# One 512-column product over w hi and w lo in the v units of a float32r decoder layer

## The chip, the cores and the metric

One core of a Trainium2 chip runs the whole kernel. The metric is device time in microseconds (us), the median of several executions of the same program; lower is better.

## What is computed

The reference is one pre-norm decoder layer on 256 tokens of width 1024, in float32 (depth is 1, so only mixer A runs; with 256 tokens there is one block, and its attention is plain causal attention with a T5 relative-position bias):

```
y = rmsnorm(h, norm_mix)
q, k, v = split(y @ w_in, 3)              # [256, 1024] @ [1024, 3072], 16 heads of 64
s = q k^T / 8 + bias(distance), causal
h = h + softmax(s) v @ w_out              # [256, 1024] @ [1024, 1024]
y = rmsnorm(h, norm_mlp)
h = h + square(relu(y @ mlp_up)) @ mlp_down   # 4096 hidden
out = rmsnorm(h, final_norm)
```

## The kernel before, in words

TensorE multiplies in float32r, a shortened float32. To keep float32 accuracy every operand of a large product is split into a high part (the value rounded to float32r) and a low part (the rest), and three products are summed: hi by hi, hi by lo, lo by hi. For the weights, 1 MB tiles are loaded into `raw` (4 slots), ScalarE copies each half of a tile to `w_hi` (`hi_tile`, line 494), and VectorE subtracts to give `w_lo` (`lo_tile`, line 672). Loads into a slot are issued by SyncE once the `lo` of the slot's previous tile is done.

The work is written out by hand, one instruction stream for each engine, tied together by semaphores. The in-projection is cut into 4 chunks of 4 heads (256 columns of each of q, k and v), numbered c = 0 to 3. Chunk 0 runs v, q, k; the others run q, k, v, with the attention of chunk c - 1 between them (scores, softmax, transposes, values). Each part of a chunk is one weight tile and two "units". The q and k units (`feature_unit`, lines 297 and 298) hold a block of weights still and stream the transposed activations `yT`, whose hi and lo halves lie side by side: for each of the 8 blocks k of 128 rows, one matmul of 512 columns (w hi against y hi and y lo) and one of 256 (w lo against y hi). The bank then holds two halves; ScalarE copies the second half to `part` (`qk_part`, line 532) and VectorE adds it to the first (`qk_sum`, line 733).

The v units (`v_unit`, lines 280 to 282) are the other way round: a block of `yT` is held still and the weights stream, 256 columns each time, so they take three matmuls for each k, all into the first 256 columns of the bank. ScalarE alone empties that bank:

```
nc.scalar.copy(v_sb[:, tb, :], bank[UNIT[tb]][:, 0:CW]).then_inc(v_ready, 1)   # v_copy, line 527
```

Both kinds of unit alternate between bank 0 and bank 1 (`UNIT`). Before a unit writes its bank, `unit_free` waits until the unit that used the bank last has been read: `v_ready` after a v unit, `qk_ready` after a q or k unit. So the first q unit of chunk 0 waits for `v_ready` to be 1, and the second for 2. The attention's `values` and the out-projection wait for `v_ready` too.

In chunk 0 TensorE runs, after the first norm: `transposes(0, 0)` (line 250), the v unit of token block 0 with `transposes(0, 1)` inside it, the v unit of token block 1, the small product of the bias table (line 423, 384 columns on 32 rows), and then four q and k units. VectorE runs there, in this order: `lo_tile(1, 0)`, `lo_tile(1, 1)`, `lo_tile(2, 0)`, the bias vector `bv_sb` (line 831, which waits for the product of line 423), `lo_tile(2, 1)`, `lo_tile(3, 0)`, `qk_sum(0, "q", 0)`, and so on. ScalarE runs `hi_tile(1, 0)`, `hi_tile(1, 1)`, `hi_tile(2, 0)`, `v_copy(0, 0)`, `hi_tile(2, 1)`, `v_copy(0, 1)`. In chunks 1 to 3 the v units come last and `scores(c)` right behind them; VectorE's next work is `add_bias` (line 742) of these scores, the start of the softmax. After chunk 3 comes the out-projection (`mix`), then the MLP, both with 512-column products at line 342 and units as above.

Of the kernel before, what the change touches and what calls it, by code (L numbers as in the profile page):

```python
# [27 lines left out]
F32R = mybir.dt.float32r  # L28
ALU = mybir.AluOpType
ACT = mybir.ActivationFunctionType  # L30

P = 128
D = 1024
T = 256
TB = T // P
KB = D // P
# [4 lines left out]
CW = 256  # L41
# [3 lines left out]
CE = D * CW // P  # L45
HALF = CE // 2
SLOTS = 4
# [10 lines left out]
HI, LO = 0, 1  # L58
# [18 lines left out]
def build(nc, x, rel_bias, norm_mix, norm_mlp, mlp_up, mlp_down, w_in, w_out, final_norm,  # L77
# [9 lines left out]
    with ExitStack() as ctx:  # L87
        def sb(name, shape, dt=F32):
            return ctx.enter_context(nc.sbuf_tensor(name, shape, dt))

        def sem(name):
            return ctx.enter_context(nc.semaphore(name))
# [3 lines left out]
        y_sb = sb("y_sb", [P, TB, D])  # L96
        yT = sb("yT", [P, KB, 2, T], F32R)
        raw = sb("raw", [P, SLOTS, CE])
        w_hi = sb("w_hi", [P, SLOTS, CE], F32R)
        w_lo = sb("w_lo", [P, SLOTS, CE], F32R)  # L100


        qT = sb("qT", [P, 2, T])
# [1 line left out]
        v_sb = sb("v_sb", [P, TB, CW])  # L105
# [4 lines left out]
        part = sb("part", [P, 2, T])  # L110
# [19 lines left out]
        bank = [ctx.enter_context(nc.psum_tensor(f"bank{i}", [P, 512], F32)) for i in range(8)]  # L130
        UNIT = [0, 1]
# [20 lines left out]
        unit_done, v_ready, part_done, qk_ready = sem("unit_done"), sem("v_ready"), sem("part_done"), sem("qk_ready")  # L152
        scores_done, biased, exp_done = sem("scores_done"), sem("biased"), sem("exp_done")
        rinv_done, normed = sem("rinv_done"), sem("normed")
        pt_done, pt_ready = sem("pt_done"), sem("pt_ready")
        pv_done, othi_done, ot_ready = sem("pv_done"), sem("othi_done"), sem("ot_ready")
        mix_done, wout_used, h_done = sem("mix_done"), sem("wout_used"), sem("h_done")
# [7 lines left out]
        def cols(slot_tensor, slot):  # L165
            return slot_tensor[:, slot, :].rearrange("p (k n) -> p k n", k=KB)

        def rows(slot_tensor, slot):
            return slot_tensor[:, slot, :].rearrange("p (k n) -> p k n", k=2)


        def unit_of(c, part):
            return 2 * IN_PARTS.index((c, part))
# [66 lines left out]
        def _(pe):  # L240
            mm = nc.tensor.matmul

            def transposes(norm, tb):

                if norm == 0 and tb == 0:
                    pe.wait_ge(ident_loaded, 16)
                for b in range(2):
                    pe.wait_ge(y_done, 2 * (norm * TB + tb) + b + 1)
                    for k in range(4):
                        last = nc.tensor.transpose(bank[NORM[tb][b]][:, k * P:(k + 1) * P],  # L250
                                                   y_sb[:, tb, (4 * b + k) * P:(4 * b + k + 1) * P], ident[:])
                    last.then_inc(yt_done, 1)

            def unit_free(n):

                if n < 2:
                    return
                c, part = IN_PARTS[n // 2 - 1]
                if part == "v":
                    pe.wait_ge(v_ready, 2 * c + n % 2 + 1)  # L260
                else:
                    pe.wait_ge(qk_ready, 4 * c + 2 * (part == "k") + n % 2 + 1)

            def v_unit(c, tb, first=False):

                n = unit_of(c, "v")
                slot = n // 2 % SLOTS
                if not first:
                    pe.wait_ge(lo_done, n + 2)
                    unit_free(n + tb)  # L270
                wh, wl = cols(w_hi, slot), cols(w_lo, slot)
                acc = bank[UNIT[tb]][:, 0:CW]
                tok = slice(tb * P, (tb + 1) * P)
                for k in range(KB):
                    if first and k % 4 == 0:
                        pe.wait_ge(ylo_done, 2 * tb + k // 4 + 1)
                        if k and tb == 0:
                            transposes(0, 1)
                        pe.wait_ge(lo_done, k // 4 + 1)
                    mm(acc, yT[:, k, HI, tok], wh[:, k, :], start=(k == 0), stop=False)  # L280
                    mm(acc, yT[:, k, HI, tok], wl[:, k, :], start=False, stop=False)  # L281
                    last = mm(acc, yT[:, k, LO, tok], wh[:, k, :], start=False, stop=(k == KB - 1))  # L282
                last.then_inc(unit_done, 1)

            def qk_unit(c, part, i):
# [129 lines left out]
            for b in range(2):  # L415
                last = mm(bank[GAIN[b]][:], ones[:], gain[0:1, b * 512:(b + 1) * 512], start=True, stop=True)
# [69 lines left out]
        def _(act):  # L486
# [9 lines left out]
            def hi_tile(t, half):  # L496

                hi(t % SLOTS, half, 16 * (t // SLOTS + 1), (unit_done, 2 * (t - SLOTS) + 2) if t >= SLOTS else None)
# [23 lines left out]
                    nc.scalar.copy(yT[:, 4 * b:4 * b + 4, HI, tb * P:(tb + 1) * P],  # L522
                                   bank[NORM[tb][b]][:].rearrange("p (k n) -> p k n", k=4)).then_inc(yhi_done, 1)

            def v_copy(c, tb):
                act.wait_ge(unit_done, unit_of(c, "v") + tb + 1)
                nc.scalar.copy(v_sb[:, tb, :], bank[UNIT[tb]][:, 0:CW]).then_inc(v_ready, 1)

            def qk_part(c, part_, i):

# [51 lines left out]
            for half in range(2):  # L582
                hi_tile(1, half)
            hi_tile(2, 0)
            v_copy(0, 0)
            hi_tile(2, 1)
            v_copy(0, 1)
            hi_tile(3, 0)
            qk_part(0, "q", 0)
            hi_tile(3, 1)  # L590
# [7 lines left out]
            for c in range(1, CHUNKS_IN):  # L598
                a, t = c - 1, 3 * c + 3
                if c == 1:  # L600
                    hi_tile(t, 0)
                    qk_part(c, "q", 0)
                softmax_exp(a, 0)
                softmax_exp(a, 1)
                softmax_exp(a, 2)
                if c > 1:
                    qk_part(c, "q", 0)
                softmax_exp(a, 3)
                if c > 1:
                    hi_tile(t, 0)  # L610
                qk_part(c, "q", 1)
                hi_tile(t, 1)
                hi_tile(t + 1, 0)
                qk_part(c, "k", 0)
                hi_tile(t + 1, 1)
                qk_part(c, "k", 1)
                out_hi(a, 0)
                out_hi(a, 1)
                hi_tile(t + 2, 0)
                hi_tile(t + 2, 1)  # L620
                v_copy(c, 0)
                v_copy(c, 1)

            a = CHUNKS_IN - 1
            for head in range(4):
# [36 lines left out]
        def _(dve):  # L662
            v = nc.vector
# [11 lines left out]
            def lo_tile(t, half):  # L675
                lo(t % SLOTS, half, 2 * t + half)
# [52 lines left out]
            def qk_sum(c, part_, i):  # L729
# [3 lines left out]
                v.scalar_tensor_tensor(dst, bank[UNIT[i]][:, 0:T], -SCALE if part_ == "q" else 1.0, part[:, i, :],  # L733
                                       ALU.mult, ALU.add).then_inc(qk_ready, 1)

            def add_bias(a, s):

                if s == 0:
                    dve.wait_ge(bias_loaded, a * 16 + 16)
                dve.wait_ge(scores_done, 4 * a + s + 1)  # L740
                for tb, own, bias in ((0, slice(0, P), slice(P, T)), (1, slice(P, 3 * P), slice(0, T))):
                    last = v.tensor_tensor_reduce(probs[:, s, own], bank[SCORE[s]][:, own], bias_sb[:, s, bias],  # L742
                                                  1.0, MASKED, ALU.add, ALU.min,
                                                  negmax[:, s, tb:tb + 1])
                last.then_inc(biased, 1)
# [80 lines left out]
            for half in range(2):  # L826
# [3 lines left out]
            dve.wait_ge(bias_summed, 1)  # L830
            v.scalar_tensor_tensor(bv_sb[:], bank[BIAS][0:HEADS, 0:BV], -1.0, fill_sb[:], ALU.mult, ALU.add
                                   ).then_inc(bias_vec, 1)
            lo_tile(2, 1)
            lo_tile(3, 0)
            qk_sum(0, "q", 0)
            lo_tile(3, 1)
# [7 lines left out]
            for c in range(1, CHUNKS_IN):  # L844
                a, t = c - 1, 3 * c + 3
                if c == 1:
                    lo_tile(t, 0)
                    softmax(a, c)
                else:
                    softmax(a)  # L850
                    qk_sum(c, "q", 0)
                softmax_rest(a)
                if c > 1:
                    lo_tile(t, 0)
                qk_sum(c, "q", 1)
                if c == 1:
                    lo_tile(t, 1)
                    qk_sum(c, "k", 0)
                    pT_copy(a, 0)
                    pT_copy(a, 1)  # L860
                    lo_tile(t + 1, 0)
                    qk_sum(c, "k", 1)
                    pT_copy(a, 2)
                    pT_copy(a, 3)
                else:
                    pT_copy(a, 0)
                    pT_copy(a, 1)
                    lo_tile(t, 1)
                    qk_sum(c, "k", 0)
                    pT_copy(a, 2)  # L870
                    pT_copy(a, 3)
                    lo_tile(t + 1, 0)
                    qk_sum(c, "k", 1)
                lo_tile(t + 1, 1)
                out_lo(a, 0)
                out_lo(a, 1)
                lo_tile(t + 2, 0)
                lo_tile(t + 2, 1)
            a = CHUNKS_IN - 1
            softmax(a)  # L880
            softmax_rest(a)
# [63 lines left out]
```

## Time and profile before

| | |
|---|---|
| median of 3 runs | 316.43 us (315.7 to 316.58) |
| span of the profiled execution, first to last instruction | 314.9 us |
| own time of the profiled execution | not given apart from its span |
| TensorE matmuls | busy 301.6 us (96% of the span), 1686 instructions |
| VectorE | busy 208.9 us (66%), 398 instructions |
| ScalarE | busy 160.7 us (51%), 293 instructions |
| DMA | 55.94 MB, mean 178 GB/s |

The span is shorter than the time by what lies around the first and the last instruction, about 1.5 us against the median. A busy time is the sum of an engine's instructions without overlaps; which of them set the end is told by the chain of waits, not by the share.

### The profile page before, as it was taken

To read this page: it belongs to the slowest core of one execution; us is meant where nothing else is said; L and a number is where in the kernel's file an instruction comes from. 1 tells how busy PE (TensorE), PEld (TensorE's weight loads), DVE (VectorE), ACT (ScalarE), POOL (GpSimd) and SP (SyncE) were. 2 spreads that over 40 slices of the span, in tenths; PEclk is the share of its full clock that TensorE was granted. 3 is DMA by queue.
4 is the path that set the end of the run, shared out by engine and by line. 5 is a ranking of instruction groups with operands and counts; after the bars stand their busy time and mean duration, and the time that the engine had idled before them with its cause. 6 is when DMAs were issued, how large, how long until landed. Compare 5 with 4: busy or idle time off the path is not lost.

```text
span 314.9 us, 4661 instructions
## 1 busy us (share of the span) xinstructions
PE 301.6 (96%) x1686; PEld 255.2 (81%) x1686; DVE 208.9 (66%) x398; ACT 160.7 (51%) x293; POOL 6.5 (2%) x14
## 2 busy tenths in 40 slices
PE   5699999999999999899999999999999999999992
PEld 2688888889889878898888888888888888888881
DVE  3677797675875849866855675585476558547554
ACT  2494584644744736454554464354446436444422
POOL 2002000000000000000000000000000000000000
PEclk9999999999999999999999999999999999999997
DMA  6989957455348034645656465645745556530003
GB/s 204 359 266 354 319 197 258 153 178 204 138 133 256 13 133 136 200 135 186 213 169 233 159 216 158 213 187 146 252 148 206 180 191 208 137 129 0 2 1 133
DMA packets 36592, 55.94 MB, mean 178 GB/s; under 512 B 1073, under 2 KB 29905, under 8 KB 36578
## 3 DMA queue, kind: packets, MB, share of 16 engines
q1 hardware_dynamic: 35586, 52.50, 50.9%
q0 software_dynamic: 992, 3.25, 3.2%
q8 instruction: 9, 0.15, 0.2%
q14 instruction: 5, 0.04, 0.0%
HBM read 54.67 MB, written 1.07 MB: 177 GB/s over the span
## 4 chain that ended last, share of the span: by engine, by line
PE 90%; DVE 4%; DMA 2%; ACT 2%; issue 1%; SPq 0%; DVEq 0%; ACTq 0%
PE bank L342 35%; PE bank L297 26%; PE bank L298 13%; PE bank L280 3%; PE bank L281 3%; PE bank L282 3%; DMA raw<-in_a_w_in_dram 2%; PE bank L380 1%; PE bank L318 1%; PE bank L381 1%; PE bank L332 1%; DVE w_lo L672 1%; PE bank L250 1%; PE bank L310 1%; PE bank L308 1%
## 5 line engine op out<-in xcount | busy, mean ns | idle before, releaser
L672 DVE TENSOR_TENSOR w_lo<-raw,w_hi 128x1024 fp32r<-128x1024 f32 x96 | 115.1, 1220 | 60.4 <-ACT w_hi L494 57.6
L297 PE MATMUL bank<-yT,w_hi 128*128 128x512 f32 x368 | 131.6, 400 | 0.1
L494 ACT CAST w_hi<-raw 128x1024 fp32r<-128x1024 f32 x95 | 96.8, 1048 | 53.1 <-PE bank L342 53.1
L298 PE MATMUL bank<-yT,w_lo 128*128 128x256 f32 x368 | 103.2, 280 | 0.0
L297 PEld LDWEIGHTS bank<-yT,w_hi 128*128 128x128 f32 x368 | 69.1, 188 | 18.4 <-issue 1.3
L342 PE MATMUL bank<-w_hi,hT 128*128 128x512 f32 x256 | 71.8, 390 | 0.0
L298 PEld LDWEIGHTS bank<-yT,w_lo 128*128 128x128 f32 x368 | 69.5, 189 | 0.5
L342 PEld LDWEIGHTS bank<-w_hi,hT 128*128 128x128 f32 x256 | 47.0, 188 | 9.7
L342 PE MATMUL bank<-w_lo,hT 128*128 128x512 f32 x128 | 40.2, 390 | 0.0
L342 PEld LDWEIGHTS bank<-w_lo,hT 128*128 128x128 f32 x128 | 24.0, 188 | 5.2
L553 ACT COPY part<-bank 128x256 f32<-128x256 f32 x30 | 11.2, 373 | 23.3 <-PE bank L298 23.3
L280 PE MATMUL bank<-w_hi,yT 128*128 128x256 f32 x64 | 19.5, 305 | 2.4 <-DVE yT L724 2.4
L342 PE MATMUL bank<-w_hi,oT 128*128 128x512 f32 x64 | 19.2, 398 | 0.0
L281 PE MATMUL bank<-w_lo,yT 128*128 128x256 f32 x64 | 18.9, 295 | 0.0
L282 PE MATMUL bank<-w_hi,yT 128*128 128x256 f32 x64 | 18.8, 294 | 0.0
L559 ACT CAST hT<-s_sb 128x256 fp32r<-128x256 f32 x32 | 13.0, 408 | 8.2 <-DVE s_sb L800 8.2
L540 ACT ACTIVATE probs<-probs,negmax 128x128 f32<-128x128 f32 (+1 forms) x32 | 14.2, 445 | 5.9 <-DVE negmax L742 5.7
L742 DVE CUSTOM_DVE_ANT_0 probs<-bank,bias_sb 128x128 f32<-128x128 f32 (+1 forms) x32 | 9.7, 349 | 9.5 <-PE bank L310 9.5
L280 PEld LDWEIGHTS bank<-w_hi,yT 128*128 128x128 f32 x64 | 13.1, 204 | 3.5 <-DVE yT L724 2.8
L795 DVE TENSOR_TENSOR z_sb<-bank,part 128x256 f32<-128x256 f32 x30 | 12.6, 421 | 4.6 <-ACT part L553 4.6
L805 DVE TENSOR_TENSOR hT<-s_sb,hT 128x256 fp32r<-128x256 f32 x32 | 13.4, 419 | 1.9 <-ACT hT L559 1.9
L800 DVE SCALAR_TENSOR_TENSOR s_sb<-z_sb 128x256 f32<-128x256 f32 x32 | 13.6, 425 | 1.1
(69 smaller groups left out, 240.4 us busy)
## 6 DMA issues: line engine op xcount, KB each, us to landing
raw<-in_mlp_up_dram SPq DMA_DIRECT2D x16, 1024.0 KB, 5.5
raw<-in_mlp_down_dram SPq DMA_DIRECT2D x16, 1024.0 KB, 4.8
raw<-in_a_w_in_dram SPq DMA_DIRECT2D x11, 1024.0 KB, 6.7
raw<-in_a_w_out_dram SPq DMA_DIRECT2D x4, 1024.0 KB, 4.8
bias_sb<-bias_by_distance POOLq DMA_DIRECT2D x4, 512.0 KB, 4.0
h_sb<-in_x_dram SPq DMA_DIRECT2D x2, 512.0 KB, 5.6
raw<-in_a_w_in_dram SPq DMA_DIRECT2D x2, 512.0 KB, 7.6
out_dram<-y_sb SPq DMA_DIRECT2D x4, 256.0 KB, 2.3
```

The costliest lines, as they stand in the source:

```text
L280: mm(acc, yT[:, k, HI, tok], wh[:, k, :], start=(k == 0), stop=False)
L281: mm(acc, yT[:, k, HI, tok], wl[:, k, :], start=False, stop=False)
L282: last = mm(acc, yT[:, k, LO, tok], wh[:, k, :], start=False, stop=(k == KB - 1))
L297: mm(dst[:], wh[:, k, own], yT[:, k, :, :], start=(k == 0), stop=False, skip_group_check=True)
L298: last = mm(dst[:, 0:T], wl[:, k, own], yT[:, k, HI, :], start=False, stop=(k == KB - 1), skip_group_check=True)
L342: last = mm(bank[ACC[tb][c]][:], lhs(l), w[:, r, c * 512:(c + 1) * 512], start=first, stop=(stop and l == LO))
L494: nc.scalar.copy(w_hi[:, slot, part_of], raw[:, slot, part_of]).then_inc(hi_done, 1)
L540: last = nc.scalar.activation(probs[:, s, own], probs[:, s, own], ACT.Exp, bias=negmax[:, s, tb:tb + 1], scale=-1.0, accum_out=rowsum[:, s ...
L559: nc.scalar.copy(hT[:, par, i, HI, :], s_sb[:, i, :]).then_inc(hhi_done, 1)
L672: v.tensor_tensor(w_lo[:, slot, own], raw[:, slot, own], f32(w_hi[:, slot, own]), ALU.subtract).then_inc(lo_done, 1)
L800: v.scalar_tensor_tensor(s_sb[:, i, :], z_sb[:, i, :], 0.0, z_sb[:, i, :], ALU.max, ALU.mult).then_inc(s_done, 1)
L805: v.tensor_tensor(hT[:, par, i, LO, :], s_sb[:, i, :], f32(hT[:, par, i, HI, :]), ALU.subtract).then_inc(hT_ready, 1)
```

## The change

In the v units the hi and the lo of a weight tile become neighbours in one tensor `w_sb`, so that a view can run over both. Of the three matmuls of each k the first two (y hi by w hi, y hi by w lo) become one of 512 columns, which puts its second half into columns 256 to 511 of the bank; the third (y lo by w hi, 256 columns) still adds to the first half. ScalarE no longer copies to `v_sb` but copies the second half of the bank to `part`, and VectorE gets a new step, `v_sum`, that adds the halves into `v_sb` and is now what raises `v_ready`.

```diff
-        w_hi = sb("w_hi", [P, SLOTS, CE], F32R)
-        w_lo = sb("w_lo", [P, SLOTS, CE], F32R)
+        w_sb = sb("w_sb", [P, SLOTS, 2, CE], F32R)
+        w_hi, w_lo = w_sb[:, :, HI, :], w_sb[:, :, LO, :]
...
+        def both(slot):
+            return w_sb[:, slot, :, :].rearrange("p l (k n) -> p k l n", k=KB)
...
-                    mm(acc, yT[:, k, HI, tok], wh[:, k, :], start=(k == 0), stop=False)
-                    mm(acc, yT[:, k, HI, tok], wl[:, k, :], start=False, stop=False)
-                    last = mm(acc, yT[:, k, LO, tok], wh[:, k, :], start=False, stop=(k == KB - 1))
+                    mm(acc[:].rearrange("p (l n) -> p l n", l=2), yT[:, k, HI, tok], wb[:, k, :, :], start=(k == 0),
+                       stop=False, skip_group_check=True)
+                    last = mm(acc[:, 0:CW], yT[:, k, LO, tok], wh[:, k, :], start=False, stop=(k == KB - 1),
+                              skip_group_check=True)
...
-            def v_copy(c, tb):
+            def v_part(c, tb):
                 act.wait_ge(unit_done, unit_of(c, "v") + tb + 1)
-                nc.scalar.copy(v_sb[:, tb, :], bank[UNIT[tb]][:, 0:CW]).then_inc(v_ready, 1)
+                nc.scalar.copy(part[:, tb, :], bank[UNIT[tb]][:, CW:2 * CW]).then_inc(vpart_done, 1)
...
+            def v_sum(c, tb):
+
+                dve.wait_ge(vpart_done, TB * c + tb + 1)
+                v.tensor_tensor(v_sb[:, tb, :], bank[UNIT[tb]][:, 0:CW], part[:, tb, :], ALU.add).then_inc(v_ready, 1)
...
             v.scalar_tensor_tensor(bv_sb[:], bank[BIAS][0:HEADS, 0:BV], -1.0, fill_sb[:], ALU.mult, ALU.add
                                    ).then_inc(bias_vec, 1)
+            v_sum(0, 0)
             lo_tile(2, 1)
+            v_sum(0, 1)
             lo_tile(3, 0)
...
                 lo_tile(t + 2, 0)
                 lo_tile(t + 2, 1)
+                v_sum(c, 0)
+                v_sum(c, 1)
```

Where the change puts `v_sum` in VectorE's queue in chunk 0. Before, VectorE's order from the third lo tile on (line 672 is `lo_tile`, 831 the bias vector, 733 `qk_sum`):

```order
17 L724 TENSOR_TENSOR yT<-bank,yT 128x4x128 [waits yhi_done] x2
18 L672 TENSOR_TENSOR w_lo<-raw,w_hi 128x1024 [waits hi_done] x3
19 L831 SCALAR_TENSOR_TENSOR bv_sb<-bank,fill_sb 16x384 [waits bias_summed,tables_loaded]
20 L672 TENSOR_TENSOR w_lo<-raw,w_hi 128x1024 [waits hi_done] x2
21 L733 SCALAR_TENSOR_TENSOR qT<-bank,part 128x256 [waits part_done]
```

After (lines are those of the changed kernel: 677 is `lo_tile`, 841 the bias vector, 744 `v_sum`, 738 `qk_sum`):

```order
17 L729 TENSOR_TENSOR yT<-bank,yT 128x4x128 [waits yhi_done] x2
18 L677 TENSOR_TENSOR w_sb<-raw,w_sb 128x1024 [waits hi_done] x3
19 L841 SCALAR_TENSOR_TENSOR bv_sb<-bank,fill_sb 16x384 [waits bias_summed,tables_loaded]
20 L744 TENSOR_TENSOR v_sb<-bank,part 128x256 [waits vpart_done]
21 L677 TENSOR_TENSOR w_sb<-raw,w_sb 128x1024 [waits hi_done]
22 L744 TENSOR_TENSOR v_sb<-bank,part 128x256 [waits vpart_done]
23 L677 TENSOR_TENSOR w_sb<-raw,w_sb 128x1024 [waits hi_done]
24 L738 SCALAR_TENSOR_TENSOR qT<-bank,part 128x256 [waits part_done]
```

The first `v_sum` stands behind three lo tiles and behind the bias vector, whose own wait is for TensorE's product after the second v unit; the second stands one lo tile further on.

On TensorE, the end of the second v unit and the first q unit of the changed kernel (284 and 286 are the two matmuls of `v_unit`, 428 the bias product, 302 and 303 the q unit):

```order
40 L286 MATMUL bank<-w_sb,yT 128x256
41 L284 MATMUL bank<-w_sb,yT 128x512
42 L286 MATMUL bank<-w_sb,yT 128x256
43 L428 MATMUL bank<-onehot_sb,rel_sb 16x384 [waits tables_loaded]
44 L302 MATMUL bank<-yT,w_sb 128x512 [waits v_ready,lo_done]
45 L303 MATMUL bank<-yT,w_sb 128x256
```

TensorE's order is the same as before but for the pairs in place of the triples; the wait for `v_ready` in front of the q unit stood there before too, and was answered by ScalarE's copy.

## Rows read from the trace of the kernel before

**Rows 1.** The page: busy time, then the chain that ended last

```profile
PE 301.6 (96%) x1686; PEld 255.2 (81%) x1686; DVE 208.9 (66%) x398; ACT 160.7 (51%) x293; POOL 6.5 (2%) x14
...
PE 90%; DVE 4%; DMA 2%; ACT 2%; issue 1%; SPq 0%; DVEq 0%; ACTq 0%
```

**Rows 2.** Waits, engine line waited for: us in total, times, longest

```profile
ACT w_hi L577 <- DMA raw<-in_a_w_in_dram: 2.6, 1, 2.6
...
PE bank L332 <- DVE pT L749: 0.4, 1, 0.4
```

**Rows 3.** Timeline of TensorE, chunk 1, v units: start us, duration us

```profile
50.64 0.28 PE L282 MATMUL bank<-w_hi,yT 128*128 128x256 f32 x1
...
56.04 0.28 PE L282 MATMUL bank<-w_hi,yT 128*128 128x256 f32 x1
```

**Rows 4.** The same view, two q and k units of chunk 1, then of chunk 2

```profile
38.30 0.28 PE L298 MATMUL bank<-yT,w_lo 128*128 128x256 f32 x1
...
43.50 0.28 PE L298 MATMUL bank<-yT,w_lo 128*128 128x256 f32 x1
...
58.10 0.28 PE L298 MATMUL bank<-yT,w_lo 128*128 128x256 f32 x1
...
63.40 0.28 PE L298 MATMUL bank<-yT,w_lo 128*128 128x256 f32 x1
```

**Rows 5.** Timeline of TensorE, chunk 0, first v unit, in brackets idle before and releaser

```profile
11.65 0.58 PE L280 MATMUL bank<-w_hi,yT 128*128 128x256 f32 x1 [2.43 <-DVE yT L724]
...
14.57 1.94 PE L250 MATMUL bank<-ident,y_sb 128*128 128x128 f32 x8
...
16.86 0.41 PE L282 MATMUL bank<-w_hi,yT 128*128 128x256 f32 x1
...
17.50 0.36 PE L282 MATMUL bank<-w_hi,yT 128*128 128x256 f32 x1
```

**Rows 6.** Timeline of VectorE from 19 to 26 us

```profile
19.52 3.50 DVE L672 TENSOR_TENSOR w_lo<-raw,w_hi 128x1024 fp32r<-128x1024 f32 x3 [1.67 <-ACT w_hi L494]
22.94 0.54 DVE L831 SCALAR_TENSOR_TENSOR bv_sb<-bank,fill_sb 16x384 f32<-16x384 f32 x1
23.40 2.34 DVE L672 TENSOR_TENSOR w_lo<-raw,w_hi 128x1024 fp32r<-128x1024 f32 x2
```

**Rows 7.** Timeline of all engines from 21 to 24 us

```profile
21.30 0.35 ACT L527 COPY v_sb<-bank 128x256 f32<-128x256 f32 x1
...
21.38 0.81 PE L423 MATMUL bank<-onehot_sb,rel_sb 32*16 32x384 f32 x2
...
22.13 0.50 PE L297 MATMUL bank<-yT,w_hi 128*128 128x512 f32 x1
```

**Rows 8.** The page, groups: count, busy us, mean ns of one

```profile
L795 DVE TENSOR_TENSOR z_sb<-bank,part 128x256 f32<-128x256 f32 x30 | 12.6, 421 | 4.6 <-ACT part L553 4.6
```

**Rows 9.** Timeline: VectorE's copy that TensorE waits for, and TensorE's start

```profile
48.43 1.01 DVE L749 COPY pT<-bank 128x384 f32<-128x384 f32 x2
...
49.50 0.65 PE L332 MATMUL bank<-pT,v_sb 128*64 128x256 f32 x4 [0.41 <-DVE pT L749]
```

**Rows 10.** Timeline from 51 to 58 us: VectorE and ScalarE around the v units

```profile
51.77 2.36 DVE L672 TENSOR_TENSOR w_lo<-raw,w_hi 128x1024 fp32r<-128x1024 f32 x2 [0.52 <-ACT w_hi L494]
57.31 0.29 DVE L742 CUSTOM_DVE_ANT_0 probs<-bank,bias_sb 128x128 f32<-128x128 f32 x1 [3.18 <-PE bank L310]
...
56.36 0.37 ACT L527 COPY v_sb<-bank 128x256 f32<-128x256 f32 x1 [2.50 <-PE bank L282]
```

**Rows 11.** Stretches: us, busy of PE, PEld, DVE, ACT, POOL, then granted clock

```profile
131.00:133.00 2.00, 0.94 (x10) 0.73 (x8) 1.26 (x3) 1.07 (x2) 0.00 (x0) 1.00 0.71 231
...
308.90:311.00 2.10, 0.21 (x1) 0.00 (x0) 1.85 (x4) 1.36 (x5) 0.00 (x0) 1.00 0.00 0
311.00:312.00 1.00, 0.00 (x0) 0.00 (x0) 0.89 (x4) 0.00 (x0) 0.00 (x0) 0.61 0.00 0
```

**Rows 12.** Timeline of TensorE, the last matmul of the program

```profile
308.73 0.39 PE L342 MATMUL bank<-w_hi,hT 128*128 128x512 f32 x1
```

More of the change, by code:

```diff
@@ L154, in build @@
         rinv_done, normed = sem("rinv_done"), sem("normed")
+        vpart_done = sem("vpart_done")
         pt_done, pt_ready = sem("pt_done"), sem("pt_ready")
@@ L270, in v_unit @@
                     unit_free(n + tb)
-                wh, wl = cols(w_hi, slot), cols(w_lo, slot)
-                acc = bank[UNIT[tb]][:, 0:CW]
+                wh, wb = cols(w_hi, slot), both(slot)
+                acc = bank[UNIT[tb]]
                 tok = slice(tb * P, (tb + 1) * P)
@@ L584, in _ @@
             hi_tile(2, 0)
-            v_copy(0, 0)
+            v_part(0, 0)
             hi_tile(2, 1)
-            v_copy(0, 1)
+            v_part(0, 1)
             hi_tile(3, 0)
@@ L620, in _ @@
                 hi_tile(t + 2, 1)
-                v_copy(c, 0)
-                v_copy(c, 1)
+                v_part(c, 0)
+                v_part(c, 1)
             a = CHUNKS_IN - 1
```

## Prediction

> **What bounds the kernel now.** I read the page first: TensorE is busy for 96% of the span and makes up 90% of the chain that ended last [rows 1]. Then the waits: once the first v unit has begun, TensorE waits for another engine only once in the whole attention half, 0.4 us in chunk 1 [rows 2]; before that unit it stood idle for 2.4 us [rows 5]. The one DMA that a working engine waits for is the first weight tile [rows 2]. So the kernel is a queue of matmuls with almost no air in it, and two things move its end: how long one matmul keeps the next from starting, and a new hole in front of one. The duration that a group reports for a matmul is no help for the first: a 256-column matmul shows 0.28 us, yet in a v unit the next one starts 0.12 us later. The prices below are therefore distances between starts in the timeline.
>
> **The three matmuls that become two.** A v unit pays, for each k, 15 steps from 50.64 to 56.04 us: 5.40 / 15 = 0.360 us for 3 x 256 columns [rows 3]. The new pair, 512 and then 256 columns, has the shape that q and k units have now. They pay 5.30 / 15 = 0.353 us in chunk 2 and 5.20 / 15 = 0.347 us in chunk 1 [rows 4]. So a k gains 0.007 to 0.013 us: the number of columns is the same, 768, and only the fixed part of one matmul goes. Chunks 1 to 3 have 3 x 2 x 8 = 48 of these steps at full pace, which is 0.3 to 0.6 us. I take 0.3, the price of the units that follow the v units directly. The operand of the long matmul now comes from two pieces of 256, 8 KB apart; no row shows such a stream, so I widen the lower end to a gain of nothing.
>
> The Trainium skill (TensorE: Matmul & The Clock Gate, the section on 56 against 53.3 ns) has a fixed cost of about 2.5 ns for each matmul at full clock. By it 48 matmuls fewer would be an estimated 0.12 us. The trace speaks for more: 7 ns and up for the one that goes [rows 3, 4].
>
> In chunk 0 the first part of the v units runs at the lower of the two paces: 0.64 us for a k, where 768 columns at 1.2 GHz are 0.64 us, until about 17.5 us [rows 5]. There is nothing to gain in the slow part, and what the rest gains is swallowed by the hole that comes next.
>
> **The new wait in chunk 0.** This is the term that decides. The first q unit writes bank 0, so it needs `v_ready` to be 1. Now this comes from ScalarE's copy, from 21.30 to 21.65 us, when TensorE still works on its bias product; the q unit starts at 22.13 us [rows 7], right after that product, and waits for nothing. After the change `v_ready` comes from `v_sum(0, 0)`, which stands in VectorE's queue behind three lo tiles and the bias vector. VectorE is the late one there: its three tiles start at 19.52, the bias vector at 22.94, and the slot behind it opens at 23.40 [rows 6]. Neither the tiles nor the bias vector get earlier by the change: the tiles wait for ScalarE's casts, and the bias vector is held by the tiles, since TensorE's product (21.38 + 0.81 = 22.19 us) is already there. `v_sum` has the shape of the MLP's sum from bank and `part`, 421 ns [rows 8]. So `v_ready` rises at 23.40 + 0.42 = 23.82. TensorE's start after such a signal: the copies of line 749 end at 48.43 + 1.01 = 49.44, the matmul starts at 49.50, so 0.06 us [rows 9]. The q unit starts at 23.88 instead of 22.13: a hole of **1.75 us**. It stands in front of everything, and TensorE has nothing else in its queue.
>
> Does anything give it back? All that follows in chunk 0 on ScalarE and VectorE hangs on the units' ends (`part_done`, then `qk_ready`), and shifts with them. `v_sum(0, 1)` comes a lo tile later, at about 25.3 us, and the second q unit does not need it before 26.7. `lo_tile(2, 1)` ends 0.34 us later, and the load that SyncE issues after it goes 0.34 us later, to be used 1.75 us later. The only wait for a DMA is at the first tile [rows 2], so no load is at its limit. The hole of 0.4 us in chunk 1 hangs on a softmax that starts from TensorE's own units, so it shifts too and closes nothing. From 22 us on, TensorE's queue carries the 1.75 us to the end.
>
> **The sums in chunks 1 to 3.** The second v copy of chunk 1 ends at 56.36 + 0.37 = 56.73. `v_sum(c, 1)` then takes VectorE to about 57.2, and VectorE's next job, the bias of the scores, starts at 57.31 because it waits for TensorE [rows 10]. `v_sum(c, 0)` falls into the 3.2 us in which VectorE idles [rows 10]. So both cost nothing, with 0.1 us of cover for the second; if that is used up, the softmax starts later by as much, not TensorE. Bank 0 is wanted only after the scores, some 3 us after `v_sum(c, 0)`, and so is the whole of `v_sb` by the out-projection, which stands behind chunk 3's scores. ScalarE's copy has the same shape as before: no change there. The MLP reads `w_hi` and `w_lo` at new addresses only.
>
> **Sum.** +1.75 - 0.3 = +1.45 us on the profiled execution: a span of 314.9 + 1.45 = 316.4. Its own time is not given; I add the difference to the median, 316.43 + 1.45 = **317.9 us**. A measurement of this kernel tells about 0.3%, or 0.95 us, from no change.
>
> **Rivals.**
> 1. *The hole also lowers TensorE's clock.* At the end of the program the granted clock still reads 1.00 up to 311 us and 0.61 in the microsecond after, so it falls to its lower level near 311.2 (0.61 is 0.22 of the time at 1 and 0.78 at one half) [rows 11], some 2 us after the last matmul ended at 308.73 + 0.39 = 309.1 [rows 12]. The hole of 1.1 us before 133 us left it at 1.00 [rows 11]. The new one, 1.7 us, lies between them, and the bias product ahead of it uses 32 rows and 16 columns of the array; counted with it the quiet stretch is 2.5 us. If the clock falls, the q units run at half pace until it rises. At the start the pace doubled at 17.5, about 3 us after the transposes at 14.6 and 6 us after the first v matmul at 11.65 [rows 5] (the clock row reads 1.00 in that stretch, so I go by the pace). Half of 3 to 6 us is lost: 1.5 to 3 us more, so 319.4 to 320.9. The Trainium skill (TensorE: Matmul & The Clock Gate, Part 1) puts it as "the default state is throttled, and activity releases the throttle"; by that rule a hole is worse than its length. Chance 0.25.
> 2. *The stall is shorter in most executions than in this profile.* The start at 22.13 hangs on when the pace doubled at 17.5. If that comes up to 3 us later in other executions, the q unit starts up to 1.5 us later before the change, and the hole shrinks by that, since VectorE's queue sets the new start. The three times spread over 0.9 us, which fits a term of that kind. Price: +0.3 to +1.1, so 316.7 to 317.5. Chance 0.2.
> 3. *The pair is cheaper than I think and the wait is not met: faster.* If two weight loads of `yT` hi in a row now cost TensorE more than the starts show, and VectorE gets to `v_sum` before 22 us, the gain alone is left. The point from which this decides is `v_ready` at 22.07 (22.13 - 0.06): VectorE would have to be 1.75 us earlier than in its rows. Then -0.3 to -0.8 us: 315.6 to 316.1. All of it is below the 0.95 us, so even this counts as faster only with luck. Chance 0.05.
> 4. *The change does not do what it says:* the long matmul over two pieces runs no faster than two of 256 columns. Then only the 0.3 us gain is gone: 318.2, inside the forecast.
>
> **How the numbers follow.** Forecast (a hole of about 1.75 us, clock kept): 0.5, 317.4 to 318.4. With the rivals at 0.25, 0.2 and 0.05, a range from 316.9 to 320.0 leaves out the far half of rival 1, the low end of rival 2 and rival 3. Slower by over 0.3% is above 317.38: the forecast, rival 1, and a little of rival 2, 0.81. Within: most of rival 2 and rival 3, 0.16. Faster: 0.03.
>
> **What would show it.** In the timeline of the changed kernel, the new line `v_sum` first starts near 23.4 us, and TensorE's next q unit near 23.9, with an idle of about 1.7 us put down to VectorE's `v_sb`. The starts of a pair in the v units lie 0.347 to 0.353 us apart. No wait for `v_sb` in chunks 1 to 3, and the bias of the scores starts at the same distance behind them. If rival 1 holds, the 256-column matmuls behind the hole lie 0.213 us apart instead of 0.12. I am wrong if the q unit starts before 23, or if TensorE has a new hole at a later chunk.

## The result, and the profile after

| | before | changed |
|---|---|---|
| median of 12 executions | 316.43 us | 317.56 us |
| lowest and highest | 315.12, 316.86 | 315.81, 320.78 |
| ratio to before, 95% interval | | 1.0047 (1.0025 to 1.0069) |
| span of the profiled execution | 314.9 us | 315.0 us |
| TensorE matmuls | 301.6 us, 1686 | 300.4 us, 1622 |

The change makes the kernel slower: by 0.5% in the ratio, which is 1.5 us, and by 1.1 us (0.4%) in the medians; 1.45 us were forecast. The ratio is taken over the fast executions, without the one at 320.78 us, and is not the quotient of the medians, which are over all 12. The two spans differ by only 0.1 us. That is no contradiction: the profiled execution of the changed kernel took 316.78 us, less than its median, and, as will be seen, started about 1 us earlier. So I compare stretches of the two traces, not the ends.

First TensorE around the end of the v units of chunk 0, changed kernel (start us, duration us; in brackets idle before and releaser; 284 and 286 are the v unit, 428 the bias product, 302 and 303 the first q unit):

```profile
10.61 0.80 PE L284 MATMUL bank<-w_sb,yT 128*128 128x512 f32 x1 [1.61 <-DVE yT L729]
...
15.23 0.50 PE L284 MATMUL bank<-w_sb,yT 128*128 128x512 f32 x1
15.57 0.28 PE L286 MATMUL bank<-w_sb,yT 128*128 128x256 f32 x1
...
19.66 0.81 PE L428 MATMUL bank<-onehot_sb,rel_sb 32*16 32x384 f32 x2
22.62 0.47 PE L302 MATMUL bank<-yT,w_sb 128*128 128x512 f32 x1 [2.14 <-DVE v_sb L744]
22.93 0.28 PE L303 MATMUL bank<-yT,w_sb 128*128 128x256 f32 x1
```

Then VectorE in the same stretch:

```profile
18.19 3.50 DVE L677 TENSOR_TENSOR w_sb<-raw,w_sb 128x1024 fp32r<-128x1024 f32 x3 [1.63 <-ACT w_sb L499]
21.60 0.54 DVE L841 SCALAR_TENSOR_TENSOR bv_sb<-bank,fill_sb 16x384 f32<-16x384 f32 x1
22.07 0.40 DVE L744 TENSOR_TENSOR v_sb<-bank,part 128x256 f32<-128x256 f32 x1
22.40 1.20 DVE L677 TENSOR_TENSOR w_sb<-raw,w_sb 128x1024 fp32r<-128x1024 f32 x1
23.53 0.41 DVE L744 TENSOR_TENSOR v_sb<-bank,part 128x256 f32<-128x256 f32 x1
```

The new wait stands where it was expected. TensorE idles 2.14 us in front of the first q unit and the releaser is `v_sum` (line 744). In VectorE's queue the sum comes 3.88 us after the first of the three lo tiles (22.07 - 18.19), as the next lo tile did before (23.40 - 19.52 = 3.88) [rows 6]: its slot was read rightly to the hundredth. It ends at 22.47, and TensorE starts at 22.62. ScalarE's copy (here 19.96 to 20.32) would have released it 2 us sooner.

The first v matmul came at 10.61 us here and at 11.65 before [rows 5], and the pace was already the full one at 15.2 instead of from 17.5. Both happen in front of the place that the change touches. They shift VectorE by 1.3 us (18.19 against 19.52), and that is why this execution ends no later.

Behind the hole, chunks 1 to 3. From the start of the first q unit to the first matmul of the out-projection it was 101.13 - 22.13 = 79.00 us before; now it is 101.25 - 22.62 = 78.63 (before, then changed):

```profile
101.13 0.74 PE L342 MATMUL bank<-w_hi,oT 128*128 128x512 f32 x2
...
101.25 0.97 PE L347 MATMUL bank<-w_sb,oT 128*128 128x512 f32 x3
```

So this pair of traces gives a gain of 0.37 us for these chunks; more traces follow below. The starts say the same (v units of chunk 1, first and last 256-column matmul):

```profile
51.11 0.28 PE L286 MATMUL bank<-w_sb,yT 128*128 128x256 f32 x1
...
56.41 0.28 PE L286 MATMUL bank<-w_sb,yT 128*128 128x256 f32 x1
```

5.30 / 15 = 0.353 us for a k, against 0.360 [rows 3], the price of the q and k units [rows 4].

The waits of the changed kernel (engine line waited for: us in total, times, longest), the lines that matter:

```profile
DVE v_sb L744 <- ACT part L532: 6.6, 3, 2.2
...
PE bank L302 <- DVE v_sb L744: 2.1, 1, 2.1
...
PE bank L337 <- DVE pT L759: 0.4, 1, 0.4
...
PE bank L302 <- DVE qT L738: 0.2, 1, 0.2
```

The last of these rows is not among the waits of before, but it is no new time. It belongs to a q or k unit behind transposes in chunk 1. From the transposes to this unit it is 44.58 - 43.62 = 0.96 us before and 45.05 - 44.08 = 0.97 us after:

```profile
43.62 0.82 PE L318 MATMUL bank<-ident,probs 128*128 128x128 f32 x6
44.58 0.47 PE L297 MATMUL bank<-yT,w_hi 128*128 128x512 f32 x1
...
44.08 0.82 PE L323 MATMUL bank<-ident,probs 128*128 128x128 f32 x6
45.05 0.47 PE L302 MATMUL bank<-yT,w_sb 128*128 128x512 f32 x1 [0.16 <-DVE qT L738]
```

TensorE waits for `v_sum` once in the whole program; the sums of chunks 1 to 3 wait for ScalarE three times, and no wait for them is in the list. In chunk 1 the second one ran from 57.13, and the bias of the scores started at 57.69, behind its end at 57.55 by 0.14 us:

```profile
57.13 0.42 DVE L744 TENSOR_TENSOR v_sb<-bank,part 128x256 f32<-128x256 f32 x1 [2.19 <-ACT part L532]
57.69 0.29 DVE L752 CUSTOM_DVE_ANT_0 probs<-bank,bias_sb 128x128 f32<-128x128 f32 x1
```

The one thing that the trace of a single execution doesn't show is the scatter. Eight of the 12 executions lie between 315.81 and 318.05 us with a mean granted clock of 0.994 to 0.999. The other four, at 319.32, 319.37, 319.39 and 320.78, have a mean of 0.991, 0.989, 0.989 and 0.986. None of the 12 executions of before lies above 316.86. The eight alone have a median of 317.16 us, 0.7 us above before; the other four bring it to 317.56. No trace was kept of one of the four.

### The profile page after: what moved, and what is told of

Its sections match the earlier page's. It is cut to its first block, busy times and chain, and to the rows that moved or that the text cites. A ratio compares the mean times of both kernels' runs of the same rounds, so it can differ in the third digit from the quotient of the medians.

```text
span 315.0 us, 4541 instructions
## 1 busy us (share of the span) xinstructions
PE 300.4 (95%) x1622; PEld 250.4 (80%) x1622; DVE 211.8 (67%) x406; ACT 160.7 (51%) x293; POOL 6.5 (2%) x14
## 4 chain that ended last, share of the span: by engine, by line
PE 88%; DVE 5%; ACT 3%; DMA 2%; issue 1%; SPq 0%; DVEq 0%; ACTq 0%
PE bank L347 35%; PE bank L302 26%; PE bank L303 13%; PE bank L284 4%; PE bank L286 2%; DVE w_sb L677 2%; DMA raw<-in_a_w_in_dram 2%; PE bank L385 1%; PE bank L323 1%; PE bank L386 1%; PE bank L337 1%; PE bank L315 1%; PE bank L254 1%; ACT w_sb L499 1%; PE bank L313 1%
## 5 line engine op out<-in xcount | busy, mean ns | idle before, releaser
L677 DVE TENSOR_TENSOR w_sb<-raw,w_sb 128x1024 fp32r<-128x1024 f32 x96 | 115.2, 1220 | 59.5 <-ACT w_sb L499 57.6
L302 PE MATMUL bank<-yT,w_sb 128*128 128x512 f32 x368 | 131.5, 400 | 2.3 <-DVE v_sb L744 2.1
L499 ACT CAST w_sb<-raw 128x1024 fp32r<-128x1024 f32 x95 | 96.8, 1048 | 53.1 <-PE bank L347 53.1
L303 PE MATMUL bank<-yT,w_sb 128*128 128x256 f32 x368 | 103.2, 280 | 0.0
L347 PE MATMUL bank<-w_sb,hT 128*128 128x512 f32 x384 | 89.9, 390 | 0.0
L302 PEld LDWEIGHTS bank<-yT,w_sb 128*128 128x128 f32 x368 | 69.1, 188 | 20.6 <-DVE w_sb L677 2.8
L347 PEld LDWEIGHTS bank<-w_sb,hT 128*128 128x128 f32 x384 | 71.0, 188 | 14.9
L303 PEld LDWEIGHTS bank<-yT,w_sb 128*128 128x128 f32 x368 | 69.5, 189 | 0.5
L284 PE MATMUL bank<-w_sb,yT 128*128 128x512 f32 x64 | 24.5, 422 | 1.7 <-DVE yT L729 1.6
L347 PE MATMUL bank<-w_sb,oT 128*128 128x512 f32 x96 | 23.2, 395 | 0.0
L284 PEld LDWEIGHTS bank<-w_sb,yT 128*128 128x128 f32 x64 | 12.6, 196 | 5.7 <-DVE yT L729 2.0
L286 PEld LDWEIGHTS bank<-w_sb,yT 128*128 128x128 f32 x64 | 12.7, 198 | 0.0
```

The lines of the kernel that those rows point to most:

```text
L284: mm(acc[:].rearrange("p (l n) -> p l n", l=2), yT[:, k, HI, tok], wb[:, k, :, :], start=(k == 0), stop=False, skip_group_check=True)
L286: last = mm(acc[:, 0:CW], yT[:, k, LO, tok], wh[:, k, :], start=False, stop=(k == KB - 1), skip_group_check=True)
L302: mm(dst[:], wh[:, k, own], yT[:, k, :, :], start=(k == 0), stop=False, skip_group_check=True)
L303: last = mm(dst[:, 0:T], wl[:, k, own], yT[:, k, HI, :], start=False, stop=(k == KB - 1), skip_group_check=True)
L347: last = mm(bank[ACC[tb][c]][:], lhs(l), w[:, r, c * 512:(c + 1) * 512], start=first, stop=(stop and l == LO))
L499: nc.scalar.copy(w_hi[:, slot, part_of], raw[:, slot, part_of]).then_inc(hi_done, 1)
```

## The experiments

Two questions were open. Is the hole the whole loss, or do the long matmul, the layout or VectorE's extra work cost too? And is the fall of the clock in a third of the executions caused by the hole? Kernels that were timed together share the executions of the kernel before: its median was 316.05 us in the first group, 316.2 in the second, 316.25 in the third. Intervals are for the ratio to it. The edits are shown against the changed kernel, that of the layout alone against the kernel before.

**Chunk 0 in the old form, chunks 1 to 3 in the new one**

```diff
-            v_unit(0, 0, True)
-            v_unit(0, 1, True)
+            v_unit_old(0, 0)
+            v_unit_old(0, 1)
...
-            v_part(0, 0)
+            v_copy(0, 0)
...
-            v_sum(0, 0)
             lo_tile(2, 1)
-            v_sum(0, 1)
```

(`v_unit_old` and `v_copy` are the unit and the copy of before; `v_sum` counts its waits from chunk 1 on.)

> Chunk 0 keeps the three 256-column matmuls and ScalarE's copy to v_sb; chunks 1 to 3 have the new form, all on the new layout. Hole theory (the cost is v_sum in VectorE's queue in front of the first q unit): no hole there, no execution above 317 us, and 0.2 to 0.4 us under the kernel before, about 316.1. Rival, the long matmul or the layout costs: slower than before, 316.8 or more. Rival, start scatter: the same as before within 0.2 us.

Measured: 315.67 us, ratio 0.9986 (0.9974 to 0.9999), highest 316.74. The loss is gone and a small gain is left, 0.4 us. So neither the layout nor the new matmul nor the three pairs of sums in chunks 1 to 3 cost anything that can be seen.

**Only chunk 0 in the new form**

```diff
-                v_unit(c, 0)
-                v_unit(c, 1)
+                v_unit_old(c, 0)
+                v_unit_old(c, 1)
...
-                v_part(c, 0)
-                v_part(c, 1)
+                v_copy(c, 0)
+                v_copy(c, 1)
...
-                v_sum(c, 0)
-                v_sum(c, 1)
```

> Only chunk 0 has the new form; chunks 1 to 3 are as before. Hole theory: the whole loss of the change is here and 0.3 us more than in the full change, since chunks 1 to 3 no longer give their gain: 1.4 to 2 us above before, about 318, with some executions near 319.5 at a lower mean clock. Rival, the loss is spread over the v units of all chunks: about a quarter of the change's loss, 316.7.

Measured: 319.07 us over 6 executions (317.29 to 319.93), ratio 1.0089 (1.0059 to 1.0118). All the loss is in chunk 0. It is more than I expected by 1 us, because three of the six lie at 319.8 to 319.9; the other three (317.29, 317.91 and 318.32) lie around the expected 318, and the median falls between the groups, where no execution is. The profiled execution (319.82 us) is of the slower three, and it shows what happens. TensorE around the hole in this variant (450 is the bias product, 324 and 325 the q unit):

```profile
21.19 0.82 PE L450 MATMUL bank<-onehot_sb,rel_sb 32*16 32x384 f32 x2
24.28 0.77 PE L324 MATMUL bank<-yT,w_sb 128*128 128x512 f32 x1 [2.27 <-DVE v_sb L770]
24.84 0.41 PE L325 MATMUL bank<-yT,w_sb 128*128 128x256 f32 x1
25.06 0.63 PE L324 MATMUL bank<-yT,w_sb 128*128 128x512 f32 x1
25.48 0.41 PE L325 MATMUL bank<-yT,w_sb 128*128 128x256 f32 x1
...
27.33 0.28 PE L325 MATMUL bank<-yT,w_sb 128*128 128x256 f32 x1
27.44 0.40 PE L324 MATMUL bank<-yT,w_sb 128*128 128x512 f32 x1
```

And the same in stretches (busy of PE, PEld, DVE, ACT and POOL, then the granted clock):

```profile
17.00:22.00 5.00, 5.00 (x26) 3.54 (x25) 3.17 (x4) 4.97 (x7) 0.00 (x0) 1.00 0.92 297
22.00:24.30 2.30, 0.03 (x2) 0.05 (x1) 2.30 (x5) 2.14 (x3) 0.21 (x1) 0.89 0.38 115
24.30:26.00 1.70, 1.70 (x5) 1.51 (x6) 1.70 (x3) 0.00 (x0) 0.28 (x1) 0.50 1.09 386
26.00:27.00 1.00, 1.00 (x5) 0.81 (x5) 0.73 (x1) 0.00 (x0) 0.00 (x0) 0.50 1.09 290
27.00:28.00 1.00, 1.00 (x6) 0.90 (x6) 0.00 (x0) 0.00 (x0) 0.30 (x1) 0.89 1.00 332
```

The granted clock falls to its lower level, 1.2 GHz, during the hole (0.89 over 2.3 us is 0.5 us at one half), stays there while the q unit runs, and returns at about 27.2. The pair takes 0.64 us instead of 0.35. From 24.28 to 27.2 that is 2.9 us at half pace, an estimated 1.5 us lost, on top of the hole. The mean clock of this execution still reads 0.994. In the other two executions near 319.9 it reads 0.994 and 0.989, so a mean at 0.994 does not exclude a fall. Part of the reason is at the end of the program. There the clock falls once more in the other traces (in that of before it reads 1.00 until 311 us and 0.61 in the microsecond after [rows 11]), but in this one, of 318.0 us, it still reads 1.00 shortly before the end:

```profile
316.00:317.00 1.00, 0.00 (x0) 0.00 (x0) 0.00 (x0) 0.00 (x0) 0.00 (x0) 1.00 1.03 385
```

So the mean counts two falls, of which only the one in the hole costs time, since TensorE has no work left at the end; the times of the executions tell more than their mean clock.

**Chunk 0's v units in banks 4 and 5**

```diff
+        VBANK = [[4, 5], UNIT, UNIT, UNIT]
...
-                if n < 2:
+                if n < 4:
                     return
...
-                acc = bank[UNIT[tb]]
+                acc = bank[VBANK[c][tb]]
...
                 act.wait_ge(unit_done, unit_of(c, part_) + i + 1)
+                if c == 0 and part_ == "q":
+                    act.wait_ge(v_ready, i + 1)
...
+                    pe.wait_ge(v_ready, 2)
                     scores(0)
```

(`v_part` and `v_sum` read `VBANK` in the same way.)

> The full change, but chunk 0's v units use banks 4 and 5, so that the q units do not wait for v_sum. Hole theory: the q unit starts right behind the bias product or behind the second lo tile of tile 1, whichever is later; at most 0.2 us of idle there; 316.0 to 316.2, and no execution with a clock below 0.994. Rival, VectorE's extra work costs by itself: still 0.5 us or more above before.

Measured: 315.7 us, ratio 0.9986 (0.997 to 1.0002), highest 316.53; that is 0.3 us under the low end of what was expected. VectorE does all the work of the change, and nothing is lost. Its trace, TensorE and VectorE (line 303 is the q unit, 748 `v_sum`):

```profile
20.87 0.81 PE L429 MATMUL bank<-onehot_sb,rel_sb 32*16 32x384 f32 x2
21.61 0.51 PE L303 MATMUL bank<-yT,w_sb 128*128 128x512 f32 x1
...
23.02 0.40 DVE L748 TENSOR_TENSOR v_sb<-bank,part 128x256 f32<-128x256 f32 x1
```

The sum is as late as ever, 1.4 us behind the start of the q unit, but TensorE no longer needs it: the q unit follows the bias product without a gap.

**The hole filled with useless matmuls**

```diff
             mm(bank[BIAS][0:HEADS, 0:BV], rel_sb[:], onehot_sb[:], start=True, stop=True).then_inc(bias_summed, 1)
+            for _ in range(7):
+                mm(bank[GAIN[1]][:], yT[:, 0, HI, 0:P], yT[:, 0, :, :], start=True, stop=True)
```

> The full change, with 7 useless 512-column matmuls into a free bank (about 1.6 us) behind the bias product, inside the hole. If the hole's idleness lowers the clock in some executions: the executions at 319.3 and above with a mean clock of 0.989 vanish, all lie between 316.5 and 318.1, and the median is the same or a little lower than the change's 317.56. If the tail has another cause, the same share (about 1 in 3) stays above 319. If fillers delay the q unit, it starts later than v_sum's end plus 0.1 us in the trace.

Measured: 317.37 us over 6 executions, 316.15 to 317.7, ratio 1.0049 (1.0032 to 1.0066). The wait is all there, but TensorE is busy in it (line 430 are the fillers):

```profile
20.24 1.88 PE L430 MATMUL bank<-yT 128*128 128x512 f32 x7
22.35 0.47 PE L302 MATMUL bank<-yT,w_sb 128*128 128x512 f32 x1 [0.23 <-DVE v_sb L746]
```

No execution is above 317.7 us. Against the variant with banks of its own, timed in the same group, the wait itself costs 317.37 - 315.7 = 1.67 us by the medians (2.0 us by the two ratios). With a third of executions affected, 6 without one are a weak proof alone; hence the next pair.

**The first sum one lo tile later, unfilled and filled**

```diff
+            lo_tile(2, 1)
             v_sum(0, 0)
-            lo_tile(2, 1)
             v_sum(0, 1)
```

Only the first sum moves: the second stood behind this lo tile already. The expectation below says "both sums", which is wrong of the edit, but TensorE's first q unit waits for the first. The filled variant has the same edit and the useless matmuls of the experiment above, 12 instead of 7.

> The full change with both sums of chunk 0 one lo tile further back. Hole theory: the q unit starts 1.13 us later in the trace, and the time is 1.1 us or more above the change's 317.5: 318.6 where the clock is kept, about 320.1 where it falls. If the fall follows the length of the idle stretch, more than half of the executions now have it. Rival, the fall is chance: still 1 in 3.

> As the variant with the sums one lo tile later, with 12 useless 512-column matmuls (2.7 us) in the hole. If idle TensorE time is what lowers the clock: all executions within about 1 us of each other, and 1.1 us above the filled hole of the change (317.37), so 318.5. The difference to the unfilled one is then the price of the clock alone. Rival, the fall has another cause: same times as unfilled.

Measured unfilled: 320.52 us (319.32 to 321.77), ratio 1.0149 (1.0118 to 1.0181). Filled with 12: 318.9 us (318.14 to 319.25), ratio 1.0087 (1.0062 to 1.0111). TensorE's start, unfilled, now waits 3 us (first row; the other two are the fillers and the q unit of the filled variant):

```profile
23.86 0.47 PE L302 MATMUL bank<-yT,w_sb 128*128 128x512 f32 x1 [2.97 <-DVE v_sb L744]
...
22.00 3.06 PE L430 MATMUL bank<-yT 128*128 128x512 f32 x12
25.23 0.47 PE L302 MATMUL bank<-yT,w_sb 128*128 128x512 f32 x1 [0.17 <-DVE v_sb L746]
```

Unfilled, the clock falls and returns (granted clock is the third number from the right):

```profile
23.00:24.00 1.00, 0.14 (x1) 0.17 (x2) 1.00 (x4) 0.00 (x0) 0.04 (x1) 1.00 1.08 381
24.00:25.00 1.00, 1.00 (x5) 0.85 (x6) 1.00 (x2) 0.00 (x0) 0.00 (x0) 0.83 1.07 366
25.00:26.00 1.00, 1.00 (x5) 0.88 (x4) 0.17 (x1) 0.00 (x0) 0.00 (x0) 0.50 1.08 374
...
28.00:29.00 1.00, 1.00 (x7) 0.88 (x7) 0.11 (x1) 0.53 (x2) 0.36 (x1) 0.97 0.58 106
```

All six unfilled executions have a mean clock of 0.985 to 0.991; none of the six filled ones is below 0.994. All six unfilled times lie above all six filled ones. So filling TensorE's idle stretch is what keeps the clock, and with the longer stretch more executions lose it: 4 of 12 with the hole of the change, 6 of 6 with one lo tile more. By the medians the clock alone costs 320.52 - 318.9 = 1.6 us, but the six fall into two groups: 319.32 to 319.91 (mean clock 0.990 to 0.991) and 321.14 to 321.77 (0.985 and 0.986), so 0.4 to 1.0 us and 2.2 to 2.9 us above 318.9. The trace is of one of the first group (319.32 us); what the second group pays more for was not traced. The wait alone grew by 1.0087 - 1.0049 = 0.38% or 1.2 us, against the 1.13 us of one lo tile. Here the fall came after TensorE had started again: the first four matmuls still ran at full pace, and the half pace began at 24.6.

**The first sum ahead of the third lo tile**

```diff
+            v_part(0, 0)
             hi_tile(2, 0)
-            v_part(0, 0)
+            v_part(0, 1)
             hi_tile(2, 1)
-            v_part(0, 1)
...
+            v_sum(0, 0)
             lo_tile(2, 0)
...
-            v_sum(0, 0)
+            v_sum(0, 1)
             lo_tile(2, 1)
-            v_sum(0, 1)
```

> The full change with ScalarE's v copies of chunk 0 one cast earlier and VectorE's first sum ahead of the third lo tile and of the bias vector (the second right behind the bias vector). Hole theory: the first q unit waits for the second lo tile plus one sum, 0.4 us of idle instead of 1.7 to 2.1; about 0.1 to 0.3 us above the variant with banks of its own, 315.8 to 316.1, and no execution at 318 or more. Rival, TensorE's start hangs on something else in chunk 0: no nearer to before than the change.

Measured: 315.69 us, ratio 0.9993 (0.9977 to 1.001), highest 316.72. The q unit waits 0.45 us:

```profile
21.87 0.47 PE L302 MATMUL bank<-yT,w_sb 128*128 128x512 f32 x1 [0.45 <-DVE v_sb L744]
```

The sum takes 0.4 us as before; its place in VectorE's queue turns a loss of 1.1 us into no loss.

**The layout alone**

```diff
-        w_hi = sb("w_hi", [P, SLOTS, CE], F32R)
-        w_lo = sb("w_lo", [P, SLOTS, CE], F32R)
+        w_sb = sb("w_sb", [P, SLOTS, 2, CE], F32R)
+        w_hi, w_lo = w_sb[:, :, HI, :], w_sb[:, :, LO, :]
```

> The kernel before, with only the new layout of w hi and w lo. All theories that put the loss into the hole: the same as before, within 0.15 us. Rival, the addresses of the streams matter: over 0.3 us away.

Measured: 316.46 us, ratio 1.0014 (1.0 to 1.0028). This was neither clearly nothing nor clearly something, so three kernels were run once more, in one group.

> The variant with chunk 0 in the old form again, now on the same chip and in the same rounds as the layout alone, so that the pair of matmuls is the only difference in chunks 1 to 3. By the starts in the trace the 48 steps give 0.3 to 0.6 us: this one under the layout alone by that. Rival, the pair gives nothing by itself and the first result was scatter: equal within 0.1 us.

> The layout alone again. If addresses cost nothing: within 0.15 us of before. If the first result (0.26 us above) was real: again 0.2 to 0.4 us above, and the pair's own gain is then larger by as much.

> The variant with banks of its own for chunk 0's v units again, same rounds. Hole theory: equal to the chunk-0-old variant within 0.2 us (chunk 0's pairs save at most 0.1 us), and 0.2 to 0.6 us under before.

Measured: chunk 0 old 315.96 us, ratio 0.9994 (0.9979 to 1.0009); layout alone 316.12 us, 1.0001 (0.9981 to 1.0021); own banks 315.47 us, 0.9976 (0.9959 to 0.9994). No cost of the layout is left to see. Two expectations missed. The pair's gain by time, chunk 0 old against layout alone, is 0.16 us and not 0.3 to 0.6; the variant with banks of its own lies 0.5 us below chunk 0 old and not within 0.2. Both are within the scatter of single medians. The variant with banks of its own has the lowest ratio of all kernels here, with 1 outside its interval in this group; in the first group 1 was inside, and it was level with chunk 0 old.

**All traces side by side**

The starts in the traces scatter less than the times. The table has the start of the first v matmul, of the first q unit and of the first matmul of the out-projection, and the two stretches between them (us):

| trace | first v | first q | out-projection | v to q | q to out-projection |
|---|---|---|---|---|---|
| before | 11.65 | 22.13 | 101.13 | 10.48 | 79.00 |
| layout alone | 11.71 | 22.00 | 100.90 | 10.29 | 78.90 |
| layout alone, again | 11.44 | 21.57 | 100.54 | 10.13 | 78.97 |
| chunk 0 old | 12.16 | 22.46 | 100.96 | 10.30 | 78.50 |
| chunk 0 old, again | 11.50 | 21.99 | 100.55 | 10.49 | 78.56 |
| own banks | 11.82 | 21.61 | 100.17 | 9.79 | 78.56 |
| own banks, again | 11.15 | 21.54 | 99.94 | 10.39 | 78.40 |
| first sum early | 11.54 | 21.87 | 100.15 | 10.33 | 78.28 |
| changed | 10.61 | 22.62 | 101.25 | 12.01 | 78.63 |
| hole filled | 10.51 | 22.35 | 100.66 | 11.84 | 78.31 |
| only chunk 0 new | 11.97 | 24.28 | 104.30 | 12.31 | 80.02 (clock fell) |
| first sum later, filled | 11.79 | 25.23 | 103.76 | 13.44 | 78.53 |

From the first v matmul to the first q unit the three traces with the hole of the change take 11.84 to 12.31 us, the seven in which TensorE does not wait for the sum 9.79 to 10.49: on average 1.8 us apart. From the first q unit to the out-projection the three with the old units in chunks 1 to 3 and a kept clock take 78.90 to 79.00 us, the eight with the new ones 78.28 to 78.63: on average 0.5 us apart, with no overlap. Hole and gain together are 1.3 us.

## Why the prediction was right, step by step

**The pair.** Right. 0.3 us were taken, 0.3 to 0.6 bounded; the profile of the changed kernel shows 0.37 us, the average over all traces is 0.5 us, and a k takes 0.353 us. The two pieces, 8 KB apart, cost no more than one: 0.353 us is the pace of the q units of chunk 2 before. With that rival 4 (no gain from the long matmul) is out. The rule of the Trainium skill (TensorE: Matmul & The Clock Gate, the section on 56 against 53.3 ns), 2.5 ns for each matmul saved and so an estimated 0.12 us, is too little here: 0.37 us over 48 steps are 7.7 ns each, and 0.5 us are 10 ns.

**The hole.** Right in place, releaser and size. Forecast: the sum in VectorE's slot behind the bias vector, TensorE 0.06 us after it, 1.75 us lost. Measured: the same slot; TensorE 0.15 us after the sum's end; 1.67 us between the filled hole and no hole by the medians, 1.8 us in the starts. That nothing gives it back holds too: the 0.4 us in chunk 1 are still there, and no wait behind the hole has gone or come. With the wait met in the trace, rival 3 is out.

The signs that the prediction named do not fit to the letter. It wanted `v_sum` near 23.4, the q unit near 23.9 and an idle of 1.7 us, and called itself wrong if the q unit started before 23; it started at 22.62, behind a `v_sum` at 22.07 and an idle of 2.14 us. These were clock times of the execution of before, and the one of the changed kernel began its v unit 1.04 us earlier. Counted from the first v matmul, 23.88 - 11.65 = 12.23 us were forecast, and 12.01 us came. A sign tied to a distance would have held; one tied to the clock time of a single execution did not allow for the start. The prediction also says that a working engine waits for only one DMA. The waits of before have more of them ahead of the v units (VectorE 3.8 us and ScalarE 2.8 us for the input, TensorE 2.4 us for the gain of the norm) and GpSimd's 4.6 us for the bias table. None of these changed the sum.

**The sums in chunks 1 to 3.** Right: no wait, and 0.14 us of cover for the second one where I had said 0.1.

**The start in the median execution.** Rival 2 said that the q unit may start up to 1.5 us later than 22.13 in other executions of before, and the hole shrink by that. No row stood behind the 3 us of later doubling that it assumed. The start of TensorE does vary (first v matmul from 10.51 to 12.16 us over the traces), but VectorE's sum moves with it (22.07 us in the changed kernel, 23.02 with banks of its own, whose first v matmul came 1.2 us later). In the seven traces without a wait for the sum the q unit starts at 21.54 to 22.46, never more than 0.33 us later than 22.13, and the stall did not shrink. So the traces do not bear the rival out; they are one execution of each kernel.

**The clock.** Rival 1, given 0.25, fits 4 of 12 executions of the changed kernel. It was priced at 319.4 to 320.9; those executions took 319.32 to 320.78. That the clock is their cause is shown by its neighbours and not in their own traces: a variant with the same hole lost it in its trace, and filling the hole kept the times together. The Trainium skill (the same page, Part 1) says that activity releases the throttle. The traces agree: with only chunk 0 new the clock fell in an idle stretch of 2.3 us and was back at 27.2, after 2.9 us of matmuls. The forecast rightly took the median to be without a fall; as a statement on the single execution, "holds or falls" was the wrong form, since both come from the same program. The prediction's bound from the end of the program, a fall some 2 us after the last matmul, was one value of a scatter: with the layout alone the last matmul ends at 308.87 and the clock reads 1.00 until 314 and 0.57 after, some 5.3 us; with the first sum early it is 4.2 us.

**The sum.** 317.9 us forecast, 317.56 measured, inside 316.9 to 320.0; slower by more than 0.3% was given 0.81, and the ratio is 1.0047. The terms were right, 1.75 - 0.3 against 1.8 - 0.5 in the traces. That the median comes as near as 0.34 us is in part luck: the forecast was for a kept clock, and the eight executions that fit this have a median of 317.16 us, 0.7 us above before and not 1.45. The filled hole, with a kept clock in all executions, lies 1.3 us above its before. Why the eight lie lower was not isolated; which executions keep the clock may go with how early they start.

## What to carry to other kernels

Ask of every semaphore that a change hands to another engine where the new instruction stands in that engine's queue, not how long it takes: 0.4 us of VectorE work cost 1.7 us because four instructions stood in front of it and a PSUM bank was waited for behind it. Where the waiting engine wants only the bank, give it another one, or move the small step ahead of the large ones; both brought the loss to nothing. When TensorE is the bound and gets a new hole, look at the spread of the executions as well as the median, since a hole of 2 us can cost more again in some of them by the clock: here those times lay 1.8 us and, once, 3.2 us above the median. And tie the signs of a prediction to distances within a trace, not to times since its start: the first v matmul alone came anywhere from 10.51 to 12.16 us.

## What the runs showed that I had not expected

The clock can fall with TensorE's idle stretch already over. With the first sum one lo tile later, the q unit started at 23.86 at full pace, and the pace halved at 24.6 while matmuls ran back to back, returning at 28.

The same program gives both: with the hole of the change (2.1 us in its profile) 4 executions of 12 lie above 319 us with a mean clock of 0.991 or less, with the same hole in chunk 0 only (2.3 us) 3 of 6 by their times, with 3.0 us 6 of 6, and with 0.45 us none of 12. Lengths between these were not tried.
